# Up-projection blocks of a decoder-step MLP by seven block products in place of eight, on one Trainium2 core

## The reference, cut to what matters

```
mod = (silu(c) @ w_ada + b_ada); sh_a, sc_a, g_a, sh_m, sc_m, g_m = split(mod, 6)
...
x  = x + g_a * (mixed @ w_out)
h2 = rms_norm(x, norm_mlp) * (1.0 + sc_m) + sh_m          # 576 x 1024
x  = x + g_m * (square(relu(h2 @ w_up)) @ w_down)         # w_up 1024 x 4096, w_down 4096 x 1024
y  = rms_norm(x, final_norm)
```

## Time and profile before

| | before |
|---|---|
| median of 3 runs (lowest to highest) | 1154.33 us (1153.62 to 1155.26) |
| the profiled execution: time | 1155.09 us |
| its span, from first to last instruction | 1153.3 us |
| PE busy | 1102.6 us (96%) |
| DVE busy | 682.0 us (59%) |
| ACT busy | 487.1 us (42%) |
| POOL busy | 87.9 us (8%) |
| mean granted PE clock | 0.984 |

### The profile page before, as it was taken

How to read it: one execution, slowest core, us unless ns; L and a number is a source line. 1 busy time by engine, 2 the same in 40 slices (tenths; PEclk the granted TensorE clock), 3 DMA queues, 4 the chain that set the end, 5 groups by cost and what they waited for, 6 DMA issues and landing times.

```text
span 1153.3 us, 21500 instructions
## 1 busy us (share of the span) xinstructions
PE 1102.6 (96%) x8725; PEld 1043.2 (90%) x8725; DVE 682.0 (59%) x1512; ACT 487.1 (42%) x851; POOL 87.9 (8%) x65
## 2 busy tenths in 40 slices
PE   5998999998999999999999998899999999999997
PEld 4797889886899999999899998899999999999997
DVE  5735554444377877778875545637354564636465
ACT  3533557466453454643354224533323323242334
POOL 2400000000000000000000011420101001010101
PEclk9899999998999999999999999999999999999998
DMA  9884333212321323221323371132232223223202
GB/s 302 278 300 146 111 111 97 88 38 73 119 93 56 97 74 113 77 76 50 100 77 94 133 259 56 50 98 74 74 110 74 74 74 105 79 74 93 74 17 83
DMA packets 108775, 120.20 MB, mean 104 GB/s; under 512 B 2692, under 2 KB 98780, under 8 KB 108389
## 3 DMA queue, kind: packets, MB, share of 16 engines
q1 hardware_dynamic: 108677, 118.83, 32.1%
HBM read 108.99 MB, written 11.80 MB: 105 GB/s over the span
## 4 chain that ended last, share of the span: by engine, by line
PE 79%; DVE 11%; ACT 5%; issue 3%; DMA 1%; POOL 0%; SPq 0%; DVEq 0%; ACTq 0%; POOLq 0%
PE PS L832 59%; PE PS L787 4%; PE PS L941 3%; DVE wR L1388 2%; PE PS L805 2%; PE PS L778 1%; DVE xhat L1356 1%; ACT wR L1071 1%; PE PS L911 1%; PE PS L889 1%; ACT pr L1198 1%; PE PS L875 1%; DMA xn<-in_x_sample 1%; PE PS L1002 1%; PE PS L754 1%
## 5 line engine op out<-in xcount | busy, mean ns | idle before, releaser
L832 PE MATMUL PS<-hR,wR 128*128 128x288 f32 x3744 | 523.7, 298 | 0.8 <-issue 0.8
L832 PEld LDWEIGHTS PS<-hR,wR 128*128 128x128 f32 x3744 | 503.0, 189 | 9.7 <-issue 8.8
L832 PE MATMUL PS<-actR,wR 128*128 128x288 f32 (+2 forms) x1920 | 260.8, 296 | 1.8 <-DVE actR L1530 1.8
L1388 DVE TENSOR_TENSOR wR<-raw,wR 128x512 fp32r<-128x512 f32 x260 | 203.1, 781 | 96.4 <-ACT wR L1071 88.8
L832 PEld LDWEIGHTS PS<-actR,wR 128*128 128x128 f32 x1920 | 257.0, 189 | 3.0 <-DVE actR L1530 2.0
L1071 ACT ACTIVATE wR<-raw 128x512 fp32r<-128x512 f32 x260 | 164.4, 632 | 142.7 <-PE PS L832 132.9
L1450 DVE CAST actR<-tmp 128x576 fp32r<-128x576 f32 x32 | 15.2, 476 | 125.8 <-ACT tmp L1182 125.8
L787 PE MATMUL PS<-wR,hR 128*128 128x256 f32 x600 | 77.5, 286 | 0.0
L787 PEld LDWEIGHTS PS<-wR,hR 128*128 128x128 f32 x600 | 73.4, 191 | 2.0 <-issue 1.7
L1405 DVE SCALAR_TENSOR_TENSOR xT<-PS,mods,xT 128x288 f32<-128x288 f32 x68 | 35.2, 518 | 62.9 <-PE PS L832 56.2
L1181 ACT ACTIVATE tmp<-PS 128x576 f32<-128x576 f32 x32 | 20.8, 652 | 120.0 <-PE PS L832 117.8
(11 more groups left out here) (219 smaller groups left out, 1070.2 us busy)
## 6 DMA issues: line engine op xcount, KB each, us to landing
raw<-in_w_in SPq DMA_DIRECT2D x30, 1024.0 KB, 5.2
raw<-in_w_up SPq DMA_DIRECT2D x16, 1024.0 KB, 5.4
raw<-in_w_down SPq DMA_DIRECT2D x16, 1024.0 KB, 5.0
mid<-in_w_ada SPq DMA_DIRECT2D x12, 1024.0 KB, 5.2
ada<-in_w_ada SPq DMA_DIRECT2D x8, 1024.0 KB, 12.5
S<-in_state_hgrn SPq DMA_DIRECT2D x8, 512.0 KB, 4.4
out_hgrn_sample<-S SPq DMA_DIRECT2D x8, 512.0 KB, 6.6
raw<-in_w_out SPq DMA_DIRECT2D x4, 1024.0 KB, 5.7
```

The costliest lines, as they stand in the source:

```text
L832: mm = pe.matmul(PS[:, 2 * x.pair + h, 0:size], weights(x, w, k, col), rhs[r], start=(k == 0 and n == 0), stop=(k == last and n == 2))
L1388: done(dve.tensor_tensor(w[:, 1, cols], raw[SLOT[SPLITS[n]]][:, cols], w[:, 0, cols].bitcast(F32), ALU.subtract), s_lo)
```

## The change

14 of the 16 up units (i = 2 to 15, `SEVEN`) are computed by seven block products in place of eight. The unit's weights are split in four blocks of 4 k x 128 features ("11", "12" for the first tile, "21", "22" for the second; the second digit is the half of k), the tokens in four blocks of 4 k x 288 ("11", "12", "21", "22": half of k, half of the tokens). With S1 = W21 + W22, S2 = S1 - W11, S3 = W11 - W21, S4 = W12 - S2 and T1 = X12 - X11, T2 = X22 - T1, T3 = X22 - X12, T4 = X21 - T2 the products are 11x11, 12x21, S2xT2, S1xT1, S3xT3, S4x22 and 22xT4, each of 12 matmuls, and the four results are sums of them.

- Tokens, once: DVE makes T1 in part 2 of up 0 and T2, T4, T3 in part 3 (`combine`); in up 1's first tile ACT makes their four high parts, DVE and POOL two low parts each (`halve`). Each is 1152 columns long.
- Weights, per unit: POOL makes four sums of 512 columns (`sums`: S1 and S3 at piece 0, S2 at piece 3, S4 at piece 5) in `tmp[2]` and `tmp[3]`; `hi` and `lo` have seven pieces of 512 in place of four, in the order 11, 12, S1, S3, S2, 22, S4. ACT's `hi` of a sum waits for POOL.
- Products in banks 4 to 7: 11x11 goes to one bank (A[0] or A[3], by turns), is copied out by ACT, and S2xT2, S3xT3 and 22xT4 are added on to it, with a copy to `tmp` after each; the others go to A[1] and A[2]. PE waits at the third, fifth, sixth and seventh product for ACT's copies.
- Epilogue per unit: ACT copies five half tiles from PSUM, DVE does three additions of 288 columns and a ReLU-and-square for each tile in one instruction (SCALAR_TENSOR_TENSOR with both inputs `tmp`), ACT rounds to `actR`, POOL makes the low part. The ReLU, the square on ACT and the cast on DVE go. ACT's first copy of a unit waits for POOL's low part of the tile before (`s_alo`), since it writes the same `tmp`.
- h2 of the MLP is made in `xhat1` in place of four rotating `tmp`, and `levels` moves to another place in SBUF.
- The load of the unit after the next is issued at the seventh piece of such a unit (part 6) where it was at the fourth (part 3).

In the diff, the object that a function calls (`pe`, `act`, `dve`, `pool`) tells whose it is; the line with `s_sum` stands in ACT's `hi`.

```diff
+SEVEN = [u for u, x in enumerate(UNITS) if x[0] == "up" and x[1] >= 2]
+PRODUCTS = [("11", "11", 0, True), ("12", "21", 1, True), ("S2", "T2", 0, False), ("S1", "T1", 2, True),
+            ("S3", "T3", 0, False), ("S4", "22", 2, False), ("22", "T4", 0, False)]
+PIECES = ["11", "12", "S1", "S3", "S2", "22", "S4"]
...
 def parts(x):
 
+    if x.u in SEVEN:
+        return 0 if x.n else len(PRODUCTS)
...
+            if x.kind == "up" and x.i == 0 and x.n == 0 and c >= 2:
+                yield ("combine", c - 2)
+            if x.kind == "up" and x.i == 1 and x.n == 0:
+                yield ("halve", c)
+            if x.u in SEVEN:
+                yield ("seven", x, c)
+            if squared is not None and c == 0:
+                yield ("squared", squared)
+                squared = None
...
             at = x.n * parts(x) + c if x.half != 1 else 4
-            if at < 4 and (x.kind, x.i) != ("up", 0) and x.split + 1 < len(SPLITS):
+            if (x.kind, x.i) != ("up", 0) and x.split + 1 < len(SPLITS) and at < CUTS[x.split + 1]:
 
                 if at == 0:
                     yield ("hi", x.split + 1)
                 yield ("lo", x.split + 1, at)
-                if at == 3 and SPLITS[x.split + 1] in AFTER:
+                if at == CUTS[x.split + 1] - 1 and SPLITS[x.split + 1] in AFTER:
                     yield ("load", AFTER[SPLITS[x.split + 1]])
...
+            def product(x, c):
+
+                j = SEVEN.index(x.u)
+                wa, tb, i, start = PRODUCTS[c]
+                bank = bank_of(x, i)
+                pe.wait_ge(s_lo, cuts(x.split, PIECES.index(wa) + 1))
...
+                if c == 0:
+                    if j >= 2:
+                        pe.wait_ge(s_kept, 5 * (j - 1))
+                elif c == 1:
+                    if j:
+                        pe.wait_ge(s_added, 3 * j - 2)
+                elif c == 3:
+                    if j:
+                        pe.wait_ge(s_added, 3 * j)
+                else:
+                    pe.wait_ge(s_kept, 5 * j + {2: 1, 4: 2, 5: 3, 6: 4}[c])
...
+                    for n, (l, r) in enumerate(((0, 0), (0, 1), (1, 0))):
+                        mm = pe.matmul(bank[:, 0:HALF], w[l], t[r], start=(start and k == 0 and n == 0), stop=(k == 3 and n == 2), skip_group_check=True)
...
+                    if b[0] == "S":
+                        act.wait_ge(s_sum, 4 * SEVEN.index(u) + ["S1", "S3", "S2", "S4"].index(b) + 1)
...
+            def seven(x, c):
+
+                j = SEVEN.index(x.u)
+                if c == 6:
+                    hi_of(x, 0)
+                if c in (1, 5):
+                    return
+                bank = bank_of(x, PRODUCTS[c][2])
+                if c == 6:
+                    act.wait_ge(s_mm, x.t + 2)
+                    act.wait_ge(s_added, 3 * j + 2)
+                else:
+                    act.wait_ge(s_prod, 6 * j + c + 1)
+                    if c == 0:
+                        act.wait_ge(s_alo, 2 * x.i - 1)
+                    if c == 3:
+                        act.wait_ge(s_alo, 2 * x.i)
+                dst = {0: (0, 0), 2: (0, 1), 3: (1, 0), 4: (1, 1), 6: (1, 0)}[c]
+                done(act.activation(halves_of(dst[0])[dst[1]], bank[:, 0:HALF], ACT.Copy), s_kept)
...
+            def combine(c):
+
+                if c == 0:
+                    dve.wait_ge(s_hhi, KT + 4)
+                    done(dve.tensor_tensor(combined("T1"), tokens_of("12"), tokens_of("11"), ALU.subtract), s_tx)
+                    return
+                dve.wait_ge(s_hhi, 2 * KT)
+                done(dve.tensor_tensor(combined("T2"), tokens_of("22"), combined("T1"), ALU.subtract), s_tx)
+                done(dve.tensor_tensor(combined("T4"), tokens_of("21"), combined("T2"), ALU.subtract), s_tx)
+                done(dve.tensor_tensor(combined("T3"), tokens_of("22"), tokens_of("12"), ALU.subtract), s_tx)
...
+            def seven(x, c):
+
+                j = SEVEN.index(x.u)
+                if c == 1:
+                    to, add, kept = halves_of(0)[0], bank_of(x, 1)[:, 0:HALF], 1
+                elif c == 5:
+                    dve.wait_ge(s_kept, 5 * j + 4)
+                    done(dve.tensor_tensor(halves_of(1)[1], halves_of(1)[1], halves_of(1)[0], ALU.add), s_added)
+                    to, add, kept = halves_of(0)[1], bank_of(x, 2)[:, 0:HALF], 2
+                if c in (1, 5):
+                    dve.wait_ge(s_prod, 6 * j + c + 1)
+                    dve.wait_ge(s_kept, 5 * j + kept)
+                    done(dve.tensor_tensor(to, to, add, ALU.add), s_added)
+                if c >= 5:
+                    if c == 6:
+                        dve.wait_ge(s_kept, 5 * j + 5)
+                    t = tmp[c - 5][:]
+                    done(dve.scalar_tensor_tensor(t, t, 0.0, t, ALU.max, ALU.mult), s_rs)
...
+            def sums(n, q):
...
+                if q == 0:
+                    pool.wait_ge(s_raw[SLOT[u]], raw_loads(u))
+                    if u == SEVEN[0]:
+                        pool.wait_ge(s_hhi, 2 * KT)
+                    else:
+                        pool.wait_ge(s_lo, cuts(SPLITS.index(SEVEN[SEVEN.index(u) - 1]) + 1))
+                    done(pool.tensor_tensor(one, cut(w, "21"), cut(w, "22"), ALU.add), s_sum)
+                    done(pool.tensor_tensor(three, cut(w, "11"), cut(w, "21"), ALU.subtract), s_sum)
+                elif q == 3:
+                    pool.wait_ge(s_lo, cuts(n, PIECES.index("S1") + 1))
+                    done(pool.tensor_tensor(one, one, cut(w, "11"), ALU.subtract), s_sum)
+                else:
+                    pool.wait_ge(s_lo, cuts(n, PIECES.index("S2") + 1))
+                    done(pool.tensor_tensor(one, cut(w, "12"), one, ALU.subtract), s_sum)
```

More of the change, by code:

```diff
@@ L421, in stage @@
             st, out = ExitStack(), []
-            for name, shape in tensors:
-                out.append(sb(name, shape, F32, st))
+            for name, shape, *dt in tensors:
+                out.append(sb(name, shape, *(dt or [F32]), st))
             st.close()
@@ L557, in decay, with cut, columns, summed @@
             return G[r % 2][:, DECAY[m]:DECAY[m] + w // m].rearrange("p (a two) -> p a two", two=2)
+        def cut(t, b):
+            k, m = 4 * (int(b[1]) - 1), P * (int(b[0]) - 1)
+            return t.rearrange("p (k c) -> p k c", c=UC)[:, k:k + 4, m:m + P]
+        def columns(t):
+            return t[:, 0:4 * P].rearrange("p (k c) -> p k c", c=P)
+        def summed(b):
+            return tmp[2 if b == "S3" else 3]
+        def piece(n, b):
+            u = SPLITS[n]
+            w = wR[split_index(n)]
+            if b in WX:
+                dst = [columns(wX[n % 2][WX.index(b)][:, part, :]) for part in range(2)]
+            else:
+                dst = [cut(w[:, part, :], "21" if b == "S1" else b) for part in range(2)]
+            return (columns(summed(b)) if b[0] == "S" else cut(raw[SLOT[u]][:], b)), dst
+        def bank_of(x, i):
+            return A[(0 if x.i % 2 == 0 else 3) if i == 0 else i]
+        def tokens_of(b):
+            k, h = 4 * (int(b[0]) - 1), int(b[1]) - 1
+            return xhat1[:, k:k + 4, h * HALF:(h + 1) * HALF]
+        def combined(b):
+            return tF[:, TX.index(b), 1, :].rearrange("p (k c) -> p k c", c=HALF)
+        def halves_of(n):
+            return tmp[n][:, 0:HALF], tmp[n][:, HALF:TOK]
         def act_tile(x):
@@ L1134, in modulate @@
                     act.wait_ge(s_vec, n * KT // 2 + k0 // 2 + 1)
-                    if k >= 4:
+                    if k >= 4 and n == 0:
                         act.wait_ge(s_hlo, n * KT + k - 3)
-                    h = tmp[k % 4]
+                    h = xhat1[:, k, :] if n else tmp[k % 4]
                     done(act.activation(h[:, 0:SEQ], xhat[n][:, k, 0:SEQ], ACT.Identity, scale=mods[:, sc + k, 0:1], bias=mods[:, sh + k, 0:1]))
                     act.wait_ge(s_hs, n * KT + k + 1)
-                    done(act.activation(hR[:, 0, k * TOK:(k + 1) * TOK], h[:], ACT.Copy), s_hhi)
+                    done(act.activation(hR[:, 0, k * TOK:(k + 1) * TOK], h if n else h[:], ACT.Copy), s_hhi)
             def evac(x):
@@ L1667, in _ @@
                     merge(*x)
+                elif ev == "combine":
+                    combine(*x)
+                elif ev == "halve":
+                    halve(*x)
+                elif ev == "seven":
+                    seven(*x)
                 elif ev == "y_put":
@@ L1728, in _ @@
                     modulate(*x)
+                elif ev == "halve":
+                    halve(*x)
+                elif ev == "lo":
+                    sums(*x)
+                elif ev == "seven" and x[1] == 6:
+                    lo_of(x[0], 0)
+                elif ev == "squared":
+                    lo_of(x[0], 1)
                 elif ev == "evac":
```

106 lines of the change are left out of this document (95 added, 11 removed).

## The result

| | before | after |
|---|---|---|
| median of 4 runs each (lowest to highest) | 1154.72 us (1153.62 to 1155.26) | 1180.39 us (1174.23 to 1182.30) |
| ratio, with its 95% interval | | 1.0203 (1.0176 to 1.0230) |
| span of the profiled execution | 1153.3 us | 1172.4 us |
| mean granted clock, by run | 0.984 (the profiled run) | 0.980, 0.973, 0.968, 0.974 |

The account below looks back on a forecast made before the run. The number of matmuls on PE was taken to bound the MLP. 1155.1 (profiled) - 22.3 + 12.3 (first-unit stand) + 2.6 (clock) + 4.9 (pair waits) = 1152.6, or 1151.8 us against the median; range 1141 to 1162.

Parts of the forecast that it names:

- the gain of 22.3 us: In 14 up units, 12 matmuls fewer each: 168 x 132.5 ns = 22.3 us, all of it on the path.
- The prices: Durations assumed for added operations, such as POOL's weight sum 1.29 us, ACT's copy of 288 columns 0.41, DVE's addition 0.46.
- the slower rival: POOL's sums take 2.0 us, pair waits 1.4 each, first seven-product unit's stand 15.1: 1159.5 us; chance 0.27.
- DVE and POOL take turns: On DVE and POOL: their operations don't overlap, so a blocked instruction waits for the other's end; strict turns were assumed.
- The entry, 12.3 us: In up 1, the first seven-product unit: PE stands 12.3 us before the third product, behind POOL's and ACT's queues.
- The clock, 2.6 us: After the 12.3 us stand in the first seven-product unit: granted clock falls, costing 2.6 us; waits of 0.7 us shouldn't.
- The pairs, 0.7 us each: Before up 2g+1's third product: PE waits 0.7 us for ACT's copy into `tmp`, seven times, 4.9 us.
- Up 2g+1 is followed by a dn unit [...] so there the same chain costs nothing: In the dn unit after up 2g+1: other banks and an `actR` group filled four units ago, so no wait.
- the sum of 1152.6: Whole profiled execution: 1155.1 - 22.3 + 12.3 + 2.6 + 4.9 = 1152.6 us.
- Taken at nothing: Other added ACT and DVE work in the MLP: covered by PE, counted as 0.
- 28 + 8 of 51 us on DVE: Per four units: DVE has 28 us of work in 51; its added part would be 8 us a group without cover.
- a wait that I missed in this order of a dozen semaphores: Aside in the 1159.5 us case: an unseen wait would act like dearer POOL sums; no place or size given.

Follow-up runs that it names:

- drop12: Kernel before with one of eight block products of each of up 2 to 15 left out and nothing added: ratio 0.9809, 1136.35 us.
- no_sums: Changed kernel without POOL's four weight sums per unit and ACT's wait for them, plain blocks used instead: ratio 1.0002, 1156.85 us.
- from4: Changed kernel with only up 4 to 15 by seven products, up 2 and 3 by eight as before: ratio 1.0093, 1166.32 us.
- other_tmp: Changed kernel with the first tile of every other seven-product unit gathered in a second buffer, idle in the MLP: ratio 1.0120.
- lo_shift: Changed kernel with DVE doing the first tile's residual of dn 2g-2 before the weight pieces of dn 2g-1: ratio 1.0025, 1160.54 us.
- late_sums: Changed kernel with POOL's S1 and S3 of up 2g+2 held until DVE has freed the first tile of dn 2g-2: ratio 1.0180.

## Why the prediction was wrong

- **What bounds the kernel, and the gain of 22.3 us**: right. drop12 shows it.
- **The prices**: right. POOL's weight sums took 1.29 us when nothing was in their way (L1946 at 924.63: 1.30) and 1.47 to 1.62 on the mean with DVE's turns; the slower rival's 2.0 us wasn't the case. ACT's copy 0.41, the long DVE pass 1.36, an addition 0.46.
- **DVE and POOL take turns**: right. What the prediction had no row for holds too. By the Trainium skill (SBUF — State Buffer, "Who interferes with whom") a DVE instruction with at most one input in SBUF, outside the two-port modes, takes no part in the lock; this trace agrees, in the timeline of the first of the seven units:

```profile
775.86 1.50 POOL L1952 TENSOR_TENSOR tmp<-raw,tmp 128x512 f32<-128x512 f32 x1 [1.78 <-DVE wx_S L1556]
776.24 0.45 DVE L1590 TENSOR_TENSOR tmp<-tmp,PS 128x288 f32<-128x288 f32 x1
776.73 1.25 DVE L1595 SCALAR_TENSOR_TENSOR tmp<-tmp 128x576 f32<-128x576 f32 x1
```

The addition with one input in PSUM and one in SBUF ran in its usual 0.45 us inside POOL's operation; the pass behind it, with `tmp` as both inputs, waited for POOL's end.
- **The entry, 12.3 us**: 11.75. Right in place, size and releaser (ACT's copy), and not by luck: POOL's S1 ended at 750.08, the token blocks at 758.55, the S4 sum at 764.47, each 0.2 to 0.4 us before the prediction's times once up 1's earlier start of 0.5 is taken off. Of its cause I had named the chain as one; no_sums and from4 part it in 5 us of token blocks and 6.7 us of sums and their queue.
- **The clock, 2.6 us**: 1.6, a term sized too large by 1.0. That the short waits leave the clock alone held for those of 0.9 us; behind the wait that I didn't have, of 2.29 to 2.36, it fell in two of six.
- **The pairs, 0.7 us each**: 0.92. Right in place and mechanism: counted from up 2g's start in group 3, 870.10, the chain's last copy began at 14.84 (884.94) for 14.6 expected. other_tmp shows that the hold over `tmp` was a little over half of the wait.
- **"Up 2g+1 is followed by a dn unit [...] so there the same chain costs nothing"**: this step failed, and with it the forecast. I asked only whether PE needs what the chain makes (`actR`, four units later). I didn't ask who stands behind the chain on the engines that carry it. On DVE that was the residual that frees a bank 6.4 us into the dn unit. I had also placed POOL's S1 and S3 of up 2g+1, but never those of the next group's up 2g+2, which fall into this dn unit and are 1.0 us of six of the waits (no_sums). It came to 7 waits, 15.5 us, where my sum had nothing, and falls of the clock behind them, 3.1 us in the trace. lo_shift shows the cause: with nothing but DVE's order changed 12.3 of the 15.5 us went. Added to the sum of 1152.6 for the profiled execution the two terms give 1171.2, of its 1174.23. The 3.0 us between are the pairs (+1.5), the new products' pace (+1.0), the kernel's end (+0.9) and the records (+1.7), less the entry (-0.55), the clock behind it (-1.0) and up 1's start (-0.5). Why the median of the four runs lies 6 us above this one stays open.
- **"Taken at nothing", with 28 + 8 of 51 us on DVE**: the share was sound and proved nothing. DVE is now 37 to 38 of 51.5 us busy, its blocked time included, a quarter is free, and PE still waits, since the free time lies elsewhere.

The slower rival (1159.5 us, 0.27) matches by sign only: the mechanism that it was priced by, a dearer POOL sum, didn't happen. Its aside, "a wait that I missed in this order of a dozen semaphores", is what came, but it had neither a place nor a price.

## What to carry to other kernels

When an edit lengthens a chain on an in-order engine, write down what stands behind it in that engine's program in the next unit too, up to the first instruction that frees a buffer of the bound engine; whether the chain's own result is urgent says nothing about that. Two engines that exclude each other have one time budget between them; moving the work to the one that does it in half the time (0.69 us for 1.29) helped a little, delaying it by a tile only moved the wait. And a wait has to be priced with what the clock does behind it.

## What the runs showed of the hardware

- A DVE instruction's record includes the time for which POOL holds it off: 1.32 us on the mean for a pass of 0.76, so DVE's busy share rises without work, here by some 31 us of 96.
- A DVE addition with one input in PSUM took 0.45 us inside a POOL operation of 1.50; with both inputs in SBUF a pass of 0.76 took 1.25 beside the same operation.
- The granted clock fell to half behind a wait of 2.3 us in some cases and in others not, with nearly equal waits and the same work around them: behind those of groups 1 and 3 in both traces of the changed kernel, of 1 and 4 in other_tmp's, and behind one of five in from4's. Behind waits of 1.4 and 1.6 us in late_sums's trace it never fell. Each fall there cost 1.4 to 1.5 us. The eight runs of this one program lie up to 10 us apart, and how much of that comes from falls behind these waits isn't shown.
